# Gate matmuls spread over the last group's samples, and first queries and keys loaded into idle weight buffers

## The chip, the cores and the metric

The kernel runs on one core of a Trainium2 chip. The metric is the device time of one execution in microseconds (us), lower is better. The engines are TensorE (PE, with its weight loads as PEld), VectorE (DVE), ScalarE (ACT), GpSimd (POOL), and SyncE (SP), which only issues DMAs here.

## The reference

One inference step of a hybrid decoder layer, for a prompt of 1024 tokens and 8 x 4 sampled tokens (1056 tokens in all). Cut to what matters:

```python
proj = jnp.einsum('btd,de->bte', x, w_in)
c_q, c_kv, k_pe, z, xbc, dt_raw, g_logits = jnp.split(proj, IN_OFFSETS, axis=-1)
q_nope, q_pe, c_kv, k_pe = mla_project(...)
attn = attend(q_nope, q_pe, c_kv, k_pe)            # 16 heads, prompt causal; samples over a paged cache
ssm_out, new_conv, new_ssm = mamba2_branch(z, xbc, dt_raw, ...)   # state-space scan, 4 groups of 8 heads
gates = jax.nn.sigmoid(g_logits + b_gate)
merged = g_a * (attn @ w_branch_a) + g_b * (ssm_out @ w_branch_b)
h = layer_norm(ALPHA * x + merged @ w_out)
y = layer_norm(ALPHA * h + swiglu_ffn(h))
```

The state-space scan goes over the prompt in chunks; for each of the 8 samples the old state is read, multiplied with its decay, added to the samples' update and written back.

## The kernel before

The program has one hand-ordered instruction stream for each engine, tied by semaphores. Stages follow one another: projections of queries, keys and values (to about 254 us), the convolution tiles (to about 552 us), the state-space scan (to about 1147 us), attention of the prompt (to about 1460 us), attention of the samples, then branches, output and feed-forward.

**Thirds.** The dense products of the stage before (z and the gate logits: 32 units of 128 output columns over 1056 tokens) are spread through the scan. Each unit is cut in three *thirds* of 352 tokens; a third is 24 matmuls of 352 columns (`third`, line 1055 on TensorE). There are 96. Six (`LEAD`) come before the first group. Each of the 4 groups has 8 chunks of 128 tokens with two thirds each (lines 1172 to 1176), and then its samples (`ssm_samples`, line 1114), where `third_with(g, q)` (line 441) says whether sample q has a third: in groups 0 to 2 all eight have, in group 3 only q = 0 and 1. Every engine asks the same function. ScalarE takes each third out of PSUM with a Silu or Sigmoid (line 1745) and stores a finished unit (528 KB, line 1750). GpSimd splits each unit's raw weights in a high and a low part one unit ahead (`split`, line 746), SP loads the raw weights four units ahead into the four slots of `raw`.

**A sample.** TensorE: a third, if there is one; 16 matmuls of 4 columns with the turned old state (line 1136); four transposes of the next old state (line 1111); four products for the update (line 1147; each is two instructions in the trace). Between them ScalarE copies the turned state out of PSUM (`s_it`, line 1775), and VectorE forms the new state (`s_new`, line 2340), which ScalarE's queue stores. The next sample's line 1136 waits for the copy, and its line 1147 for the new state. SP loads the old states of q = 4 to 7 when the new states of q = 0 to 3 are out (line 567).

**Into attention.** When all 74 units are done (`unit_done` 74, line 620), SP loads the first two pairs of heads: for each pair two rotary key rows (`d_kr`, 128 KB each), two queries (384 KB), two keys and two values (256 KB each). The buffers `qb`, `kb`, `vb` (lines 402 to 410) lie over `xhi` and `xlo`, the tokens that every third reads. TensorE waits for `kr_full` (line 1185) and `head_full0`, computes the first pair's eight scores (line 1251), four before ScalarE has to read one (`probs`, line 1821). ScalarE first waits until all of its stores of the scan have landed (lines 1808 to 1815) and then signals `ssm_over`. DMA queue q1 is SP's, q10 ScalarE's. After the loop over pairs, SP loads the first weights of the branches into `raw` (line 682).

Of the kernel before, what the change touches and what calls it, by code (L numbers as in the profile page):

```python
# [16 lines left out]
D_MODEL, SEQ, NB, NT = 1024, 1024, 8, 4  # L17
# [3 lines left out]
HEADS, NOPE, ROPE, VH = 16, 64, 32, 64  # L21
QH = NOPE + ROPE
# [3 lines left out]
DI, SH, SP_, SG, SN = 2048, 32, 64, 4, 128  # L26
# [72 lines left out]
LEAD = 6  # L99
# [49 lines left out]
def build(nc, a, o, stop=99, debug=None):  # L149
# [22 lines left out]
    def sem(name):  # L172
        if name in taken:
            return sem(taken[name][0])
        if name not in sems:
            sems[name] = nc.alloc_semaphore(name)
        return sems[name]
# [22 lines left out]
    base = -(-nc.sbuf_base // 64) * 64  # L200
# [52 lines left out]
    d_kr = scratch("d_kr", [ROPE, TOK])  # L253
# [14 lines left out]
    ar = Arena(floor)  # L268
# [133 lines left out]
    qb, kb, vb = [], [], []  # L402
    ar = Arena(low)
    for pp in range(2):
        qb.append([ar(f"qb{pp}{h}", [QH, SEQ]) for h in range(2)])
        kb.append([ar(f"kb{pp}{h}", [QH, SEQ]) for h in range(2)])
        if pp == 1:
            assert ar.at <= at_wkv
            ar = Arena(at_kvt)
        vb.append([ar(f"vb{pp}{h}", [P, SEQ // P, VH]) for h in range(2)])  # L410
# [29 lines left out]

    def third_with(g, q):

        return g < SG - 1 or q < 8 - LEAD

    def step_of(g, c):

# [11 lines left out]
    def _(sp):  # L458
# [17 lines left out]
        def columns(n):  # L476
            return lambda r: r.rearrange("p (k n) -> p k n", n=n)

        def tile_of(w, col, n=P):
            return w[:, bass.ds(col, n)].rearrange("(k p) n -> p k n", p=P)  # L480
# [136 lines left out]
            return  # L617


        sp.wait_ge(sem("unit_done"), 74)  # L620
        for pp in range(2):
            for h in range(2):
                sp.dma_start(kb[pp][h][NOPE:QH, :], d_kr[:, 0:SEQ]).then_inc(sem("kr_full"), k["kr_full"].adds(16))

        one = lambda d, h: d[bass.ds(h, 1)].rearrange("a p n -> (a p) n")

        def queries_keys(pp, pair):
            for h in range(2):
                for dst, src in ((qb[pp][h][:, :], one(d_q, pair * 2 + h)[:, 0:SEQ]), (kb[pp][h][0:NOPE, :], one(d_k, pair * 2 + h))):
                    sp.dma_start(dst, src).then_inc(sem(f"head_full{pp}"), k[f"head_full{pp}"].adds(16))  # L630

        def head_values(pp, pair):
            for h in range(2):
                sp.dma_start(vb[pp][h][:, :, :].rearrange("p a n -> p (a n)"), one(d_v, pair * 2 + h)).then_inc(sem(f"head_full{pp}"), k[f"head_full{pp}"].adds(16))

        for pp in range(2):
            queries_keys(pp, pp)
            head_values(pp, pp)
        sp.wait_ge(sem("ssm_over"), 1)

        with nc.allow_non_contiguous_dma(reason="a page number for each quarter page, 4 KB in all"):
# [11 lines left out]
        with looped(sp, HEADS // 4 - 1, {k["s_ready"]: 32, k["o_ready"]: 4} | pairs(k, {"head_full": 96})) as i:  # L653
            for pp in range(2):
                sp.wait_ge(sem("s_ready"), k["s_ready"].next(16))
                queries_keys(pp, i * 2 + 2 + pp)
                sp.wait_ge(sem("o_ready"), k["o_ready"].next(2))
                head_values(pp, i * 2 + 2 + pp)
        if stop < 7:
# [10 lines left out]
        def gate_up(blk):  # L670
            return [[(columns(P), tile_of(w, blk * 256 + j * P))] for j in range(2) for w in (w_g, w_u)]

        def next_weights(n):
            for _ in range(n):
                weights(to_load.pop(0))
# [3 lines left out]
        for g in range(2):  # L679
            to_load += row_units(w_a, g * 512, 512, 256)  # L680
        to_load += [[(columns(P), tile_of(w_o, e * P))] for e in range(KT)] + gate_up(0)
        next_weights(4)
        sp.wait_ge(sem("olat_read"), 1 + NB - 1)

# [192 lines left out]
    def _(pe):  # L877
# [304 lines left out]
        for c in range(3):  # L1182
            pe.wait_ge(sem(f"third_free{c}"), k[f"third_free{c}"].next())
        pe.wait_ge(sem("xd_ready"), k["xd_ready"].next())
        pe.wait_ge(sem("kr_full"), k["kr_full"].next(64))
        pe.wait_ge(sem("bf_ready"), k["bf_ready"].next(2))

        def scores(pp, G, i):

            q, h, b = 4 * G + 3 - i // 2, i % 2, i % 2  # L1190
            if G == 0 and i == 0:
                pe.wait_ge(sem(f"head_full{pp}"), k[f"head_full{pp}"].next(96))
            first_bank = 2 * b + (i // 2 % 2 if G == 0 else 0)
            pe.wait_ge(sem(f"s_read{b}"), k[f"s_read{b}"].held() - (1 if G == 0 and i >= 2 else 0))
            length = (q + 1) * P
            for c in range(0, length, 512):
                w = min(512, length - c)
                pe.matmul(ps[:, first_bank + c // 512, 0:w], qb[pp][h][:, q * P:(q + 1) * P], kb[pp][h][:, c:c + w], start=True, stop=True)  # L1198
            at = q * P
            last = pe.matmul(ps[:, first_bank + at // 512, at % 512:at % 512 + P], ident_b[:, :], after_b[:, :], start=False, stop=True,  # L1200
                             skip_group_check=True)
            last.then_inc(sem("s_ready"), k["s_ready"].adds(1))
# [46 lines left out]
        per_two = {k["s_ready"]: 32, k["n_ready"]: 32, k["o_ready"]: 4} | pairs(k, {"head_full": 96, "s_read": 16, "pt_read": 24,  # L1249
                   "t_ready": 24, "o_read": 2})  # L1250
        for i in range(8):
            scores(0, 0, i)
        pe.wait_ge(sem("bt_read"), k["bt_read"].next())
        pe.wait_ge(sem("cb_read"), k["cb_read"].next())
        pe.wait_ge(sem("y_out"), k["y_out"].next())
# [1586 lines left out]
```

## Time and profile before

| | us |
|---|---|
| median of 3 runs | 3004.88 |
| lowest, highest | 2998.44, 3005.58 |
| profiled execution | 2995.18 |
| its span (first to last instruction) | 2993.3 |
| mean granted TensorE clock | 0.968 |

```profile
PE 2855.1 (95%) x18828; PEld 2562.1 (86%) x18828; DVE 1532.1 (51%) x2076; ACT 771.4 (26%) x1197; POOL 1024.6 (34%) x587
```

TensorE is busy 95% of the span. That is a mean over stages; the change touches the 600 us of the scan and its passage into attention, so it is those stretches that have to be read: which engine has idle time there, what ended it, and what clock TensorE was granted (1.00 is 2.4 GHz, 0.50 is 1.2 GHz).

### The profile page before, as it was taken

How to read it: one execution, taken by the hardware profiler on the slowest of the kernel's cores; microseconds unless marked ns; L12 is line 12 of the kernel's file. 1: busy time of each engine (PE TensorE's matmuls, PEld its weight loads, DVE VectorE, ACT ScalarE, POOL GpSimd, SP SyncE). 2: the span in 40 equal slices, each digit the busy share in tenths (PEclk: the TensorE clock that was granted, in tenths of full speed). 3: DMA queues.
4: the chain of work that ended last, by engine and by line, in shares of the span. 5: the costliest groups of instructions: out<-in, count | busy, mean ns of one | idle time of the engine just before them, and what ended most of it. 6: DMA issues, size and time to landing. Idle time of an engine off the chain costs nothing.

```text
span 2993.3 us, 45619 instructions
## 1 busy us (share of the span) xinstructions
PE 2855.1 (95%) x18828; PEld 2562.1 (86%) x18828; DVE 1532.1 (51%) x2076; ACT 771.4 (26%) x1197; POOL 1024.6 (34%) x587
## 2 busy tenths in 40 slices
PE   8899999999999998999999989999899999999996
PEld 7789999899989995555666689999799999999996
DVE  2774887664746554555344357865652222222227
ACT  1211221353535443555332222110220000000004
POOL 3543333332323322444211123444233333333330
PEclk9999999999999997999899989999899999999997
DMA  4154223574755535222334243353111111111101
GB/s 139 46 158 148 79 86 110 160 188 132 185 144 166 148 114 152 64 63 74 138 127 189 93 146 136 109 180 111 54 36 50 43 47 46 43 50 43 44 28 58
DMA packets 314166, 308.87 MB, mean 103 GB/s; under 512 B 31813, under 2 KB 272714, under 8 KB 311498
## 3 DMA queue, kind: packets, MB, share of 16 engines
q1 hardware_dynamic: 252008, 194.57, 22.9%
q10 hardware_dynamic: 58394, 73.89, 7.2%
q0 software_dynamic: 3584, 37.75, 3.3%
q8 instruction: 144, 2.36, 0.3%
q14 instruction: 36, 0.29, 0.0%
HBM read 227.96 MB, written 78.20 MB: 102 GB/s over the span
## 4 chain that ended last, share of the span: by engine, by line
PE 67%; DVE 12%; issue 10%; POOL 5%; ACT 4%; DMA 1%; SPq 0%; ACTq 0%; POOLq 0%; DVEq 0%
PE ps L908 41%; PE ps L1068 10%; POOL pr L854 4%; DVE cv L2199 3%; PE ps L1348 2%; PE ps L1324 2%; PE ps L1304 2%; DVE cv L2193 1%; PE ps L1147 1%; PE ps L1101 1%; DVE cv L2201 1%; PE ps L1105 1%; PE ps L979 1%; PE ps L1094 1%; ACT so L1696 1%
## 5 line engine op out<-in xcount | busy, mean ns | idle before, releaser
L751 POOL TENSOR_TENSOR whi<-raw,cst 128x1024 fp32r<-128x1024 f32 x160 | 312.0, 1950 | 1162.9 <-PE ps L908 959.9
L753 POOL TENSOR_TENSOR wlo<-raw,whi 128x1024 fp32r<-128x1024 f32 x160 | 431.2, 2695 | 12.6
L908 PE MATMUL ps<-ahi,whi 128*128 128x352 f32 x1728 | 376.4, 326 | 5.7 <-issue 3.5
L908 PE MATMUL ps<-alo,whi 128*128 128x352 f32 x1728 | 375.7, 326 | 0.0
L908 PE MATMUL ps<-ahi,wlo 128*128 128x352 f32 x1728 | 372.8, 324 | 0.0
L908 PEld LDWEIGHTS ps<-ahi,whi 128*128 128x128 f32 x1728 | 294.9, 190 | 7.4 <-issue 4.7
L908 PEld LDWEIGHTS ps<-ahi,wlo 128*128 128x128 f32 x1728 | 297.0, 190 | 0.0
L908 PEld LDWEIGHTS ps<-alo,whi 128*128 128x128 f32 x1728 | 295.5, 188 | 0.0
L1068 PE MATMUL ps<-xhi,whi 128*128 128x352 f32 x768 | 257.0, 335 | 0.6 <-ACT xraw L1693 0.4
L1068 PE MATMUL ps<-xhi,wlo 128*128 128x352 f32 x768 | 248.7, 324 | 0.0
L1068 PE MATMUL ps<-xlo,whi 128*128 128x352 f32 x768 | 248.6, 324 | 0.0
L854 POOL TENSOR_TENSOR pr<-pr,rowinv 128x384 f32<-128x384 f32 (+7 forms) x128 | 145.4, 1146 | 201.1 <-DVE rowinv L2402 201.1
L1198 PE MATMUL ps<-kb,qb 96*128 96x512 f32 (+3 forms) x384 | 160.4, 536 | 10.3 <-ACT pr L1827 6.9
L2397 DVE TENSOR_REDUCE negmax<-ps 128x1 f32<-128x384 f32 (+7 forms) x128 | 97.0, 758 | 136.9 <-PE ps L1200 136.2
L908 PE MATMUL ps<-xhi,whi 128*128 128x352 f32 x720 | 159.5, 330 | 6.0 <-ACT xraw L1693 3.9
L2583 DVE TENSOR_TENSOR mm<-ps,mm 128x1056 f32<-128x1056 f32 x80 | 100.6, 1258 | 116.3 <-PE ps L908 116.3
L908 PE MATMUL ps<-xlo,whi 128*128 128x352 f32 x720 | 158.1, 328 | 0.0
L908 PE MATMUL ps<-xhi,wlo 128*128 128x352 f32 x720 | 156.7, 327 | 0.0
L1198 PEld LDWEIGHTS ps<-kb,qb 96*128 96x128 f32 x384 | 65.1, 197 | 104.4 <-issue 83.5
L1068 PEld LDWEIGHTS ps<-xhi,whi 128*128 128x128 f32 x768 | 145.0, 189 | 9.2 <-issue 6.8
L1068 PEld LDWEIGHTS ps<-xlo,whi 128*128 128x128 f32 x768 | 145.1, 189 | 0.0
L1068 PEld LDWEIGHTS ps<-xhi,wlo 128*128 128x128 f32 x768 | 145.0, 189 | 0.0
(363 smaller groups left out, 5143.8 us busy)
## 6 DMA issues: line engine op xcount, KB each, us to landing
raw<-in_w_in SPq DMA_DIRECT2D x61, 512.0 KB, 5.1
s_a<-d_acum SPq DMA_DIRECT2D x32, 512.0 KB, 7.1
d_xbc<-so ACTq DMA_DIRECT2D x24, 528.0 KB, 2.7
gt<-d_g SPq DMA_DIRECT2D x24, 528.0 KB, 3.7
raw<-in_w_ffn_gate SPq DMA_DIRECT2D x22, 512.0 KB, 3.8
raw<-in_w_ffn_up SPq DMA_DIRECT2D x22, 512.0 KB, 3.8
raw<-in_w_ffn_down SPq DMA_DIRECT2D x22, 512.0 KB, 3.6
d_z<-zo ACTq DMA_DIRECT2D x16, 528.0 KB, 4.9
```

The costliest lines, as they stand in the source:

```text
L751: pool.tensor_tensor(whi[s][:, :], raw[:, u], ones[:, 0:1].broadcast_to([P, UNIT]), ALU.mult).then_inc(sem("unit_hi"), k["unit_hi"].adds(1))
L753: pool.tensor_tensor(wlo[s][:, :], raw[:, u], whi[s][:, :].bitcast(F32), ALU.subtract).then_inc(sem("unit_split"), k["unit_split"].adds(1))
L854: pool.tensor_tensor(pr[G][i][:, :], pr[G][i][:, :], rowinv[:, n:n + 1].broadcast_to([P, length]), ALU.mult).then_inc(sem("n_ready"), k["n ...
L908: last = pe.matmul(ps[0:m, 3 * b + c, 0:width], w(j), x[:, j, at:at + width], start=i == 0, stop=i == n - 1)
L1068: last = pe.matmul(ps[:, c, 0:CH], w[u % SPLIT][:, j * P:(j + 1) * P], x[:, j, c * CH:(c + 1) * CH], start=i == 0, stop=i == 3 * KT - 1)
L1198: pe.matmul(ps[:, first_bank + c // 512, 0:w], qb[pp][h][:, q * P:(q + 1) * P], kb[pp][h][:, c:c + w], start=True, stop=True)
L1304: last = pe.transpose(ps[:, 4 + i % 3, r * P:(r + 1) * P], src, ident)
L1324: last = pe.matmul(half(c, s), qcur[b][:, j, :], kvt[:, j, 4 * g:4 * g + 4, :].rearrange("p r n -> p (r n)"), start=False, stop=j == 1, sk ...
L1348: last = pe.matmul(ps[64 * s:64 * s + 64, 7, 0:KL], prt[:, 4 * c + r, 64 * s:64 * s + 64], kvb[b][:, 8 * r + 4 * s + c, :], start=r == c = ...
L2199: dve.scalar_tensor_tensor(out=cv[b][:, 0:SEQ], in0=xraw[b][:, j:j + SEQ], scalar=tap(j), in1=cv[b][:, 0:SEQ], op0=ALU.mult, op1=ALU.add). ...
L2397: dve.tensor_reduce(negmax[:, n:n + 1], src, AX, ALU.max, negate=True).then_inc(sem("m_ready"), k["m_ready"].adds(1))
L2583: dve.tensor_tensor(thirds(mm[:, e]), out3(b), thirds(mm[:, e]), ALU.add).then_inc(sem(f"res_free{b}"), k[f"res_free{b}"].adds(1))
```

## The change

In each of the groups 0 to 2 sample q = 3 has no third any more. The last group has thirds at q = 1, 3, 5, 6 and 7 in place of 0 and 1. The total remains 96, and the numbering of thirds in groups 1 to 3 shifts by one, two and three.

The query and key buffers of pair 0 are placed at the base of the memory, over the four slots of `raw`, and are filled when the last unit of weights has been split (`unit_split` 74) rather than when the last unit is done. The values of pair 0 and everything of pair 1 still wait for `unit_done` 74. TensorE's first eight scores wait for pair 0's rotary keys, queries and keys (`kr_full` 96), and for the values only after them. SP waits for all scores of pair 6 before it loads the first branch weights into `raw`.

```diff
-        qb.append([ar(f"qb{pp}{h}", [QH, SEQ]) for h in range(2)])
-        kb.append([ar(f"kb{pp}{h}", [QH, SEQ]) for h in range(2)])
+        qk = ar if pp else Arena(base)
+        qb.append([qk(f"qb{pp}{h}", [QH, SEQ]) for h in range(2)])
+        kb.append([qk(f"kb{pp}{h}", [QH, SEQ]) for h in range(2)])
...
     def third_with(g, q):
-        return g < SG - 1 or q < 8 - LEAD
+        return q != 3 if g < SG - 1 else q in (1, 3, 5, 6, 7)
...
-        sp.wait_ge(sem("unit_done"), 74)
-        for pp in range(2):
+        def rotary_keys(pp, name):
             for h in range(2):
-                sp.dma_start(kb[pp][h][NOPE:QH, :], d_kr[:, 0:SEQ]).then_inc(sem("kr_full"), k["kr_full"].adds(16))
+                sp.dma_start(kb[pp][h][NOPE:QH, :], d_kr[:, 0:SEQ]).then_inc(sem(name), k[name].adds(16))
...
-        for pp in range(2):
-            queries_keys(pp, pp)
-            head_values(pp, pp)
+        sp.wait_ge(sem("unit_split"), 74)
+        rotary_keys(0, "kr_full")
+        queries_keys(0, 0, "kr_full")
+        sp.wait_ge(sem("unit_done"), 74)
+        head_values(0, 0)
+        rotary_keys(1, "head_full1")
+        queries_keys(1, 1, "head_full1")
+        head_values(1, 1)
         sp.wait_ge(sem("ssm_over"), 1)
...
+        sp.wait_ge(sem("s_ready"), k["s_ready"].next(16))
         next_weights(4)
...
-        pe.wait_ge(sem("kr_full"), k["kr_full"].next(64))
+        pe.wait_ge(sem("kr_full"), k["kr_full"].next(96))
...
         for i in range(8):
-            scores(0, 0, i)
+            scores(0, 0, i, True)
+        pe.wait_ge(sem("head_full0"), k["head_full0"].next(32))
```

## Rows read from the trace of the kernel before

**Rows 1.** Windows: length; PE, PEld, DVE, ACT, POOL busy; clock, DMA share, GB/s.

```profile
964.00:1022.00 58.00, 58.00 (x486) 53.71 (x485) 20.80 (x52) 16.92 (x25) 10.63 (x7) 1.00 0.40 121
1108.00:1158.00 50.00, 43.50 (x311) 34.82 (x309) 15.05 (x49) 8.34 (x14) 0.00 (x0) 0.67 0.62 166
```

**Rows 2.** Timeline of TensorE, last group's samples: start, length, engine, line, operation.

```profile
1110.37 0.41 PE L1068 MATMUL ps<-xhi,whi 128*128 128x352 f32 x1
...
1114.40 0.64 PE L1136 MATMUL ps<-s_e,s_it 128*64 128x4 f32 x16
...
1116.63 0.43 PE L1068 MATMUL ps<-xhi,whi 128*128 128x352 f32 x1
...
1120.42 0.32 PE L1068 MATMUL ps<-xhi,wlo 128*128 128x352 f32 x1
1120.67 0.64 PE L1136 MATMUL ps<-s_e,s_it 128*64 128x4 f32 x16
...
1122.91 0.64 PE L1136 MATMUL ps<-s_e,s_it 128*64 128x4 f32 x16
...
1125.53 1.02 PE L1136 MATMUL ps<-s_e,s_it 128*64 128x4 f32 x16
...
1137.53 1.02 PE L1136 MATMUL ps<-s_e,s_it 128*64 128x4 f32 x16
...
1142.91 2.04 PE L1147 MATMUL ps<-s_bt,s_u 32*128 32x128 f32 x8 [0.35 <-DVE s_new L2340]
```

**Rows 3.** Timeline of ScalarE at the last group's first sample.

```profile
1110.65 0.60 ACT L1775 ACTIVATE s_it<-ps 128x512 f32<-128x512 f32 x1 [1.05 <-PE ps L1111]
```

**Rows 4.** Windows around two falls of the clock, columns as in rows 1.

```profile
449.43:451.59 2.16, 0.01 (x1) 0.03 (x1) 0.11 (x1) 1.61 (x2) 2.08 (x2) 1.00 0.35 139
451.59:452.66 1.07, 1.07 (x7) 1.07 (x8) 1.07 (x1) 0.00 (x0) 1.07 (x1) 1.00 0.57 225
452.66:456.00 3.34, 3.34 (x13) 3.34 (x13) 3.31 (x7) 0.00 (x0) 1.03 (x1) 0.50 0.36 83
...
1122.90:1125.00 2.10, 1.95 (x27) 1.71 (x27) 1.51 (x5) 0.26 (x1) 0.00 (x0) 1.00 0.32 133
1125.00:1129.50 4.50, 4.50 (x32) 3.73 (x30) 1.51 (x5) 0.94 (x2) 0.00 (x0) 0.51 0.68 186
```

**Rows 5.** Timeline of the DMA issues: first head load, last store of y.

```profile
1131.20 1.96 SPq L623 DMA_DIRECT2D kb<-d_kr  x4
...
1146.78 0.37 ACTq L1768 DMA_DIRECT2D d_y<-s_y  x1
```

**Rows 6.** Timeline of the passage into attention.

```profile
1147.46 2.05 PE L1198 MATMUL ps<-kb,qb 96*128 96x512 f32 x2 [2.52 <-DVE after_b L2377]
...
1156.09 1.28 ACT L1827 ACT_TABLE_LOAD   x1 [15.85 <-DMA d_y<-s_y]
...
1158.21 1.22 PE L1198 MATMUL ps<-kb,qb 96*128 96x256 f32 x2 [3.69 <-ACT pr L1827]
```

**Rows 7.** DMA traffic in 1132.7:1155.7, in 1135:1140 and in 1140:1144.

```profile
DMA packets 5102, 5.80 MB, mean 252 GB/s; under 512 B 880, under 2 KB 3819, under 8 KB 5099
...
DMA packets 338, 1.11 MB, mean 221 GB/s; under 512 B 68, under 2 KB 68, under 8 KB 338
...
DMA packets 1009, 1.28 MB, mean 320 GB/s; under 512 B 72, under 2 KB 646, under 8 KB 1007
```

**Rows 8.** Landings by line: queries and keys (L630), then y (L1768, two stores).

```profile
DMA to landing us min/median/max: 5.7/8.9/12.7
...
DMA to landing us min/median/max: 2.3/5.6/8.8
```

**Rows 9.** First branch weights: their issue on SP, and the splits on GpSimd.

```profile
1391.70 2.29 SPq L473 DMA_DIRECT2D raw<-in_w_branch_b  x4
...
L751 POOL TENSOR_TENSOR whi<-raw,cst x6: 1892/1894/1911, 1664.2 to 1794.9; 128x1024 fp32r<-128x1024 f32 x6
```

More of the change, by code:

```diff
@@ L617, in _, with queries_keys @@
             return
-        sp.wait_ge(sem("unit_done"), 74)
-        for pp in range(2):
+        one = lambda d, h: d[bass.ds(h, 1)].rearrange("a p n -> (a p) n")
+        def rotary_keys(pp, name):
             for h in range(2):
-                sp.dma_start(kb[pp][h][NOPE:QH, :], d_kr[:, 0:SEQ]).then_inc(sem("kr_full"), k["kr_full"].adds(16))
-        one = lambda d, h: d[bass.ds(h, 1)].rearrange("a p n -> (a p) n")
-        def queries_keys(pp, pair):
+                sp.dma_start(kb[pp][h][NOPE:QH, :], d_kr[:, 0:SEQ]).then_inc(sem(name), k[name].adds(16))
+        def queries_keys(pp, pair, name):
             for h in range(2):
                 for dst, src in ((qb[pp][h][:, :], one(d_q, pair * 2 + h)[:, 0:SEQ]), (kb[pp][h][0:NOPE, :], one(d_k, pair * 2 + h))):
-                    sp.dma_start(dst, src).then_inc(sem(f"head_full{pp}"), k[f"head_full{pp}"].adds(16))
+                    sp.dma_start(dst, src).then_inc(sem(name), k[name].adds(16))
         def head_values(pp, pair):
@@ L655, in _ @@
                 sp.wait_ge(sem("s_ready"), k["s_ready"].next(16))
-                queries_keys(pp, i * 2 + 2 + pp)
+                queries_keys(pp, i * 2 + 2 + pp, f"head_full{pp}")
                 sp.wait_ge(sem("o_ready"), k["o_ready"].next(2))
@@ L1184, in _, with scores @@
         pe.wait_ge(sem("xd_ready"), k["xd_ready"].next())
-        pe.wait_ge(sem("kr_full"), k["kr_full"].next(64))
+        pe.wait_ge(sem("kr_full"), k["kr_full"].next(96))
         pe.wait_ge(sem("bf_ready"), k["bf_ready"].next(2))
-        def scores(pp, G, i):
+        k["head_full1"].n = 32
+        def scores(pp, G, i, first=False):
             q, h, b = 4 * G + 3 - i // 2, i % 2, i % 2
-            if G == 0 and i == 0:
+            if G == 0 and i == 0 and not first:
                 pe.wait_ge(sem(f"head_full{pp}"), k[f"head_full{pp}"].next(96))
```

## The prediction

> **What bounds the kernel now.** I read three things in this order. First the busy time and granted clock by stage. In the samples of the third group TensorE is busy throughout and the clock is full; the first two groups' read alike, so one row stands for the three. In the last group's 50 us TensorE is busy 43.5 and the mean clock is 0.67 [rows 1]. So the other groups' samples are bound by TensorE, and the last group's are not. Second the timeline of that last stretch. A sample with a third takes 6.26 us from third to third (1110.37 to 1116.63), one without takes 2.62 (1122.91 to 1125.53) while the clock is full and 4.00 (1125.53 to 1137.53 is three) after it has fallen [rows 2]. The clock fell about 1125.1, some 4.5 us after the last third's matmuls ended, while TensorE was busy nearly all the time with short matmuls [rows 2, 4]. Third what ends the wait between the samples and attention. The first scores start at 1147.46 and fill the free banks; the next ones start at 1158.21, behind ScalarE's exponentials. ScalarE had idled 15.85 us until 1156.09, released by the landing of the last store of y, issued at 1146.78 and 8.8 us under way [rows 5, 6, 8]. That store lands so late because the DMA engines are full with the head loads and the stores of new states: 5.80 MB from 1132.7 to 1155.7 [rows 7]. Thus the end of the stage is set by a drain of DMA, not by the scores' own operands.
>
> **The thirds taken from the other groups.** Three thirds leave. At q = 3 of groups 0 to 2 a block of 6.26 becomes one of 2.62: 3 x 3.64 = 10.9 us off TensorE's path [rows 2]. What is late next in such a block is VectorE's new state, for which the update's matmuls wait some tenths of a microsecond, and ScalarE's copy of 0.60; both are in the 2.62 already [rows 2, 3]. The splits on GpSimd and the unit loads on SP move by one or two thirds with the count, but both are made three thirds ahead of use and there are two or three thirds' time under them; I cost them at nothing. If that cover were gone, a split would stand on the path, by its first half of 1.89 us [rows 9] and an estimated 2 to 3 for the second.
>
> **The thirds given to the last group.** It had thirds at q = 0 and 1 and gets them at 1, 3, 5, 6, 7. Before, the stretch from the first third (1110.37) to the end of the last update (1142.91 + 2.04 = 1144.95) is 34.6 us [rows 2]. After, at full clock: q = 0 has no third to hide the copy of the turned state, which ends at 1110.65 + 0.60 = 1111.25, so 0.9 us of stall [rows 3], then 2.23 for its own matmuls (1114.40 to 1116.63); four blocks with a third, 4 x 6.26 = 25.0; two without, 5.2; and the last one, 4.03 for the third and about 1.7 for the rest: 39.1 us. That is 4.5 more, and 10.9 - 4.5 = 6.4 us earlier at the end of the samples. In the old group's time scale the last third ends at 1147.8 and the samples at 1149.5; 10.9 is to be taken off both.
>
> **The first pair's loads.** Keys and queries of pair 0 (1.57 MB) go to the buffers of raw weights, after the last split instead of after the last unit. SP gets there only after the wait for the new state of q = 3, where it stood until 1131.20 in the kernel before too [rows 5]. In the changed kernel that is over 20 us ahead of the scores, against landings of 12.7 us at most [rows 8], so these loads are hidden. They compete with the stores of new states, whose buffers are used again only four samples later, 2 x 6.26 + 2 x 2.62 = 17.8 us. Nothing of this is gained by itself: the scores did not wait for their operands before either.
>
> **What is late next.** The other ten loads (values of pair 0, everything of pair 1: 2.62 MB) now wait for the last third, which is the last sample's. Behind that wait on SP's queue stand these ten and the page numbers; the first is needed by the first weighing, more than 10 us later, so the loads themselves are hidden. But they fall together with the last gate store (0.54 MB), the last new state (0.26) and y (0.07), all of which ScalarE waits for before its first exponential: 3.49 MB. From issue to flow was 1.5 us (1131.20 to 1132.7). The rate was 5.80 / 23.0 = 0.252 MB/us over the whole stretch, 0.222 from 1135 to 1140 and 0.32 from 1140 to 1144 [rows 7]. The first is nearest, since it too mixes loads and stores: 13.9 us, with ends of 10.9 and 15.7. So the drain ends at 1147.8 + 1.5 + 13.9 = 1163.2, less 10.9 = 1152.3, against 1146.78 + 8.8 = 1155.6 [rows 5, 8]: **3.3 us earlier**, with ends at 6.3 and 1.5. Half of the gain at the samples' end is lost to a longer drain. After it everything runs as before. The new wait of SP ahead of the weights of the next stage costs nothing: those loads were issued at 1391.70 and first split at 1664.2 [rows 9]; the wait puts them at most some tens of us later.
>
> **The clock.** This is the price that the trace does not settle. Taking a third away leaves a stretch of one sample's rest, 2.2 us, and a whole bare sample, 2.6: 4.8 us between the matmuls of two thirds. There are six: one in each of the groups 0 to 2, and before q = 1, 3 and 5 of the last (the first is 1.7 us of opening work plus 3.1). The 2.2 us stretches never cost the clock in the groups 0 to 2 [rows 1]. The one long stretch of the old kernel did, after 4.5 us [rows 2, 4]. Elsewhere the clock fell soon after a pause of only 2.16 us, though full-width matmuls had begun again 1.07 us before [rows 4]. So each of the six can fall, and none must. A fall is followed by 3.34 us at the half clock in the second case, in which 13 wide matmuls ran; at the third's pace (4.03 / 24 = 0.168 us) they take 2.2 us, so it lost 1.2; half of the stretch, 1.7, is the most. I take 1.4. The cost lies between 0 and 6 x 1.7 = 10.2 us; with half of the six falling it is 4.2.
> On the clock the Trainium skill ("TensorE: Matmul & The Clock Gate", section "Why this matters for your kernels") asks only that there be no idle gaps of some length between bursts. By that the six stretches, which are busy with short matmuls, would keep the full clock, and the sum would be that of the second case below. The trace speaks against reading it so: TensorE was busy 1.95 of 2.10 us just before the fall at 1125.1 [rows 4].
>
> **The sum.** -10.9 + 4.5 + 3.1 (longer drain) + 4.2 (clock) = +0.9 us. The profiled execution took 2995.18 us (span 2993.3, 1.9 around it), so 2996.1 by its own time. It lies 9.7 below the median of the three runs, 3004.88; I put the same difference on the median: **3005.8**.
>
> **The rivals.**
> - *Forecast, 0.50*: some of the six stretches lose the clock, the drain takes most of the rest: -1 to +4 around +0.9.
> - *The clock holds in all six, 0.22*: -3.3 us (-6.3 to -1.5 by the rates), 3001.6. For it: the short stretches of three groups held [rows 1]. Against it: the one of like length fell.
> - *The last stores are not held up by the loads, 0.12*: y is issued at 1149.5 + 1.8 - 10.9 = 1140.4 and lands 2.3 us later, as the one before it did [rows 8]; 1142.7 against 1155.6 is -12.9, so 2992.0. For it: fewer stores of new states are queued before it. Against it: in 1135 to 1140 the engines moved loads only, 338 packets, with stores outstanding [rows 7].
> - *Slower, 0.11*: all six stretches fall and the clock stays down through the whole third that follows, which then takes 4.03 us more. Six of these are 24.2, less 3.3: +20.9, 3025.8. It decides from four of the six on (16.1 - 3.3 = +12.8). For it: after the fall at 1125.1 the clock was still low at 1129.5, with TensorE busy throughout. Against it: it came back after 3.34 us of wide matmuls [rows 4].
> - *The change doesn't do what it says, 0.05*: the copy and update chains of the last group are slower with thirds between them, or the first pair's loads displace the states of the last samples, and the gain at the samples' end is gone: +3 to +6, about 3009. For it: the bare samples wait for VectorE. Against it: that wait is 0.35 us [rows 2].
>
> **The numbers.** What this kernel's measurement can tell from no change is about 0.3%, 9 us. The range reaches to half of the early-store case and takes in the milder part of the slow one: 2992 to 3014, which leaves out about 0.06 below and 0.10 above. Faster by over 0.3%: the early stores 0.12, the best end of the others 0.05, together 0.17. Slower: the slow case 0.11 and 0.03 of the forecast's and the last case's upper ends, 0.14. Same: 0.69.
>
> **What would show it.** At q = 3 of groups 0 to 2, blocks of 2.6 us between 6.26 ones; in the last group a stretch of 39 us from the first state copy to the last update, with full clock but for short falls; the drain step, in a y store that takes 10 us or more and ScalarE's first exponential some 13 us behind the last update (11 before). The clock step is wrong if the granted clock is 1.00 in all four groups' samples, or low for whole samples. The prediction fails if ScalarE's release comes within 6 us of the last update, or if chunk steps of the groups get longer than before, for which I found no reason.

## The result

| | time (us) | executions |
|---|---|---|
| before | 3003.09 (2991.70 to 3011.88) | 20 |
| after | 3014.35 (3007.76 to 3021.12) | 20 |
| after / before | 1.0037 [1.0028, 1.0047] | |

The change makes the kernel slower by 0.37%, some 11 us. 3005.8 was forecast, 0.9 us more than before; the measured time lies 0.35 us beyond the upper end of 3014, and slower had a chance of 0.14. The profiled execution of after took 3013.98 us (span 3012.2, mean clock 0.968).

The stretch that the change touches is read best by cutting it at the groups: each group's samples, from the turning of the state to the start of the last update, and the chunks between them. These are the windows of after in that cut (length; PE, PEld, DVE, ACT, POOL busy; granted clock, DMA share, GB/s). The rows of 46.90, 48.50, 50.00 and 44.00 are samples:

```profile
676.60:723.50 46.90, 46.75 (x413) 42.79 (x410) 15.71 (x41) 13.29 (x21) 10.57 (x5) 1.00 0.37 114
723.50:817.20 93.70, 91.93 (x709) 83.62 (x707) 66.66 (x95) 51.43 (x64) 33.99 (x18) 1.00 0.73 182
817.20:865.70 48.50, 48.34 (x414) 44.36 (x412) 19.25 (x41) 15.02 (x22) 14.80 (x7) 0.96 0.39 121
865.70:962.20 96.50, 93.46 (x706) 85.14 (x705) 65.85 (x95) 52.95 (x64) 34.05 (x18) 0.98 0.65 171
962.20:1012.20 50.00, 49.84 (x413) 45.78 (x410) 16.71 (x41) 13.94 (x21) 9.60 (x5) 0.93 0.38 117
1012.20:1105.40 93.20, 91.96 (x708) 83.65 (x707) 66.05 (x95) 52.86 (x64) 38.19 (x20) 1.00 0.55 146
1105.40:1149.40 44.00, 42.91 (x358) 39.14 (x356) 11.63 (x37) 7.99 (x14) 0.00 (x0) 0.88 0.43 121
```

And the same cut of a second profile of before (b1 below), of which the first two chunk stretches and the last group are enough; the samples of its other groups took 50.7 or 50.8 each at a clock of 1.00:

```profile
728.50:820.80 92.30, 91.90 (x707) 83.58 (x706) 66.80 (x95) 51.40 (x63) 38.91 (x20) 1.00 0.71 183
...
871.50:965.20 93.70, 91.94 (x709) 83.62 (x707) 66.56 (x95) 52.87 (x64) 38.18 (x20) 1.00 0.68 181
...
1108.40:1142.30 33.90, 33.39 (x286) 29.36 (x284) 11.63 (x37) 6.44 (x11) 0.00 (x0) 0.75 0.56 153
```

Three things are to be seen. The first group's samples show the gain without disturbance, 46.9 for 50.8; the next two have a lower clock and give part of it back. The last group takes 10 us more (44.0 for 33.9), at a clock of 0.88. And the chunks, in which nothing was changed, take 93.7 and 96.5 for 92.3 and 93.7.

The clock falls where the six stretches without wide matmuls are. In the last group of after, windows between the falls:

```profile
1105.40:1110.20 4.80, 4.02 (x54) 3.28 (x52) 1.47 (x3) 1.75 (x3) 0.00 (x0) 1.00 0.19 55
1110.20:1113.60 3.40, 3.40 (x13) 3.40 (x13) 1.51 (x5) 0.00 (x0) 0.00 (x0) 0.50 0.15 41
...
1115.70:1120.50 4.80, 4.64 (x58) 3.90 (x57) 1.51 (x5) 1.75 (x3) 0.00 (x0) 1.00 0.02 4
1120.50:1123.90 3.40, 3.40 (x13) 3.40 (x13) 1.51 (x5) 0.00 (x0) 0.00 (x0) 0.50 0.70 196
```

TensorE is busy 4.64 of 4.80 us with short matmuls, the clock then falls to its lower level (0.50, 1.2 GHz) just as the third's wide matmuls begin, and a good half of the third's 24 run at it. It is the same picture as in [rows 4], with 13 matmuls in the low stretch there and here; [rows 4] had it behind a pause. In this execution five of the six stretches ended so; the first one alone did not.

The passage into attention, timeline of ScalarE and TensorE in after:

```profile
1149.41 1.15 PE L1153 MATMUL ps<-s_bt,s_u 32*128 32x128 f32 x8
...
1152.39 0.49 ACTq L1777 DMA_DIRECT2D d_y<-s_y  x1
...
1159.85 1.28 ACT L1836 ACT_TABLE_LOAD   x1 [10.34 <-DMA d_y<-s_y]
...
1161.97 1.22 PE L1206 MATMUL ps<-kb,qb 96*128 96x256 f32 x2 [2.02 <-ACT pr L1836]
```

The last update starts 6.5 us later than in before ([rows 2], 1142.91), ScalarE is released 3.8 us later ([rows 6], 1156.09). The release is still set by y's landing.

### The profile page after: what moved, and what is told of

It reads as the page before. It is cut to its first block, busy times and chain, and to the rows that moved or that the text cites. A ratio compares the mean times of both kernels' runs of the same rounds, so it can differ in the third digit from the quotient of the medians.

```text
span 3012.2 us, 45617 instructions
## 1 busy us (share of the span) xinstructions
PE 2863.7 (95%) x18828; PEld 2563.1 (85%) x18828; DVE 1534.2 (51%) x2076; ACT 771.4 (26%) x1197; POOL 1023.4 (34%) x587
## 4 chain that ended last, share of the span: by engine, by line
PE 68%; DVE 12%; issue 10%; POOL 5%; ACT 3%; DMA 2%; SPq 1%; ACTq 0%; POOLq 0%; DVEq 0%
PE ps L914 40%; PE ps L1074 11%; POOL pr L860 4%; DVE cv L2208 3%; PE ps L1357 2%; PE ps L1333 2%; PE ps L1313 2%; PE ps L1107 1%; PE ps L1153 1%; DVE cv L2202 1%; PE ps L1111 1%; PE ps L1100 1%; DVE cv L2210 1%; PE ps L985 1%; ACT so L1705 1%
```

## The experiments

All profiles were cut in the same way. "Samples" are the four groups' samples, "chunks" the three stretches between them, "to last update" their sum, and "to samples' attention" the time from the last update's start to the first matmul of the attention of the samples. Times are medians, but for those marked (one), which are single executions. Ratios, with their 95% intervals, are to before, run at the same time on the same chip: e1 to e4, b1 to l2, c1 to c4, and d1 with d2 ran together. A ratio is an estimate of its own and differs by up to 0.0013 from the quotient of the two medians. The stretches are lengths and not points in time, because executions differ ahead of them too: the first group's samples open at 677.8 us in before and at 668.5 in p1, though the work up to there is the same.

| kernel | samples | chunks | to last update | to samples' attention | time (us) | ratio |
|---|---|---|---|---|---|---|
| before | 50.8 50.8 50.8 34.1 | 92.6 93.5 92.6 | 465.1 | 349.3 | 3003.09 | 1 |
| after | 46.9 48.4 50.0 44.0 | 93.7 96.6 93.2 | 472.8 | 346.4 | 3014.35 | 1.0037 [1.0028, 1.0047] |
| e1 after, shifted | 46.9 46.9 50.0 44.0 | 93.4 97.9 93.5 | 472.6 | 349.7 | 3014.75 | 1.0049 [1.0031, 1.0067] |
| e2 thirds alone | 48.5 49.8 50.0 45.5 | 93.6 96.3 93.6 | 477.3 | 357.8 | 3023.78 | 1.0072 [1.0052, 1.0091] |
| e3 buffers alone | 50.8 50.8 50.8 34.8 | 92.6 93.8 92.5 | 465.9 | 348.9 | 3004.66 | 1.0005 [0.9992, 1.0019] |
| e4 after again | 48.5 50.0 46.9 42.4 | 95.7 95.0 93.6 | 472.1 | 349.5 | 3008.57 (one) | |
| b1 before again | 50.8 50.8 50.8 33.9 | 92.3 93.7 92.5 | 464.6 | 349.8 | 3004.89 (one) | |
| p1 pieces, 21 and 15 | 46.9 46.9 46.9 38.5 | 93.5 96.9 93.3 | 463.0 | 351.1 | 3004.21 | 1.0007 [0.9996, 1.0017] |
| l1 old thirds, late loads | 50.8 50.8 50.8 33.5 | 92.6 95.5 93.0 | 466.9 | 344.6 | 2999.29 | 0.9989 [0.9973, 1.0005] |
| l2 after, late loads | 46.9 48.4 50.0 43.9 | 93.6 96.5 93.5 | 472.9 | 343.2 | 3005.62 | 1.0012 [0.9997, 1.0026] |
| c1 after, unit loads moved | 46.9 46.9 46.9 45.6 | 93.7 96.1 93.3 | 469.4 | 350.3 | 3009.73 | 1.0021 [1.0006, 1.0036] |
| c2 pieces, 24 and 6, late loads | 50.8 50.8 50.8 27.0 | 92.4 93.6 92.8 | 458.0 | 343.4 | 2989.63 | 0.9957 [0.9941, 0.9972] |
| c3 pieces, 21 and 15, late, moved | 46.9 46.9 46.9 38.5 | 93.3 96.4 93.2 | 462.1 | 343.8 | 2994.82 | 0.9972 [0.9957, 0.9987] |
| c4 before, third profile | 50.8 50.8 50.8 34.0 | 92.3 93.6 92.7 | 464.8 | 349.4 | 3003.03 (one) | |
| d1 pieces, 24 24 15 15, late | 50.8 50.8 39.7 38.5 | 92.5 93.4 93.2 | 458.9 | 344.1 | 2986.68 | 0.9944 [0.9923, 0.9965] |
| d2 pieces, 24 and 6 | 50.8 50.8 50.8 27.0 | 92.4 93.5 92.7 | 457.9 | 350.0 | 2993.95 | 0.9976 [0.996, 0.9992] |

**Each half alone, and a false lead.** Between the first profile of before and that of after, a second difference stood out far behind the change: in the attention of the samples, blocks of 64 short products took 1.28 us before and 2.86 after, in six of eight sequences. TensorE's instructions of after are one fewer, so a theory was that the whole stream's position matters. e1 shifts it back by one instruction, a wait that is long satisfied:

```diff
+        pe.wait_ge(sem("ident_full"), 16)
         pe.wait_ge(sem("late_full"), k["late_full"].next(96))
```

> The changed kernel with one idle wait more on TensorE, on a semaphore that is long there, just ahead of the attention of the samples; it puts every later TensorE instruction back by one place in its stream, to where it stood in the kernel before. Theory P (place in the instruction stream): the blocks of 64 short products of keys with rotary queries, which took 2.86 us each in the changed kernel's profile and 1.28 before, are back at 1.28; eight of them give back 8 x 1.6 = 12.8 us, so about 3014.4 - 12.8 = 3001.6, within 3 us of the kernel before. Rival M (the buffers' new place in memory, or the loads' new order, slow these products): nothing changes, some 11 us above the kernel before, blocks still 2.86 us.

e2 is before with the new distribution of thirds, e3 is after with the old one:

```diff
-        return g < SG - 1 or q < 8 - LEAD
+        return q != 3 if g < SG - 1 else q in (1, 3, 5, 6, 7)
```

> The kernel before with the new spread of thirds alone; buffers and order of loads as before, all twenty head loads (4.2 MB) behind the last third, and TensorE's instructions as many as before. Theory P: the short products stay at 1.28 us. The passage into attention gets later: in the changed kernel's profile attention's first exponential stood 5 us behind that of the kernel before (the 1.2 us by which that run was ahead at the start counted in); another 1.57 MB in the drain at 0.25 MB/us make 6 more, so +11 us in all, 3014. If the drain isn't what sets the end (rival), +3 to +6. A gain in the three bare blocks of 3.6 us each less what falls of the clock cost.

> The changed kernel with the old spread of thirds: first pair's queries and keys in the idle weight buffers, thirds at 0 to 7 in groups 0 to 2 and at 0 and 1 in the last. TensorE has the same one instruction fewer as the changed kernel. Theory P: the short products take 2.86 us, 12.8 us more in all; the passage into attention is as before, the head loads being gated by the same state store, so +12 to +13 us, 3016. Theory M expects the same here. If neither holds (a matter of one execution), 0.

e4 is after, unchanged:

> The changed kernel once more, for a second profile. If the slow short products belong to the program, all eight blocks take 2.86 us again; if to the execution, 1.28 in some. The falls of the clock in the six long stretches should come at other places, some three to five of them again.

The position theory fell: e1 has the blocks at 2.8 us, and the time of after. e2, e3 and e4 have the long blocks too, whatever their time. What was left was that the first profile of before had caught an uncommon execution, and a second profile of before (b1) was to settle it.

> The kernel before, unchanged, profiled a second time. In the first profile of it the blocks of 64 short products between the new states' samples in the stage after attention took 1.28 us in the sequences; in the kernel after, in both halves of the change alone and in the repeat of after they took 2.8 us in most. Theory 1 (a matter of the execution, not of the code): here too most take 2.8 us, that stage is some 10 us longer than in the first profile, and the profiled execution is close to the median, about 3003 us. Theory 2 (the change causes it): they take 1.28 us again in all, and the profiled execution is about 2995 us. In both the last update ends 572.6 us after the transposes that open the convolution.

It did. The same block, in the first profile and in the second one of before (timeline of TensorE; the 1.28 and 2.86 us count from the block's start to the next instruction, which is at 1521.73 and at 1523.17):

```profile
1520.44 1.35 PE L1319 MATMUL ps<-kpt,qcur 32*64 32x128 f32 x64
```

```profile
1520.31 1.31 PE L1319 MATMUL ps<-kpt,qcur 32*64 32x128 f32 x45
1521.95 0.46 PE L1319 MATMUL ps<-kpt,qcur 32*64 32x128 f32 x5 [0.33 <-issue]
1522.71 0.53 PE L1319 MATMUL ps<-kpt,qcur 32*64 32x128 f32 x14 [0.30 <-issue]
```

With the same code, the block is now broken twice by pauses for which the profile shows no cause. b1's execution took 3004.89 us and the first one 2995.18, and up to the samples' attention they agree within 0.5 us. c4 repeats it:

> The kernel before, profiled a third time, beside these three. Theory of two kinds of execution: the 64 short products in the attention of the samples take either 1.28 or 2.86 us in nearly all six inner places, the execution is 8 to 10 us shorter with the former, and everything up to that stage is the same within 1 us of the earlier two profiles when counted from the opening of the first group's samples (465 us to the last update).

It took 3003.03 us, with blocks of 2.86 and 464.8 us to the last update. The common execution is the one with pauses. The pauses are not all that makes executions differ: p1's profiled one took 2991.46 us, 13 below its median, and has them. Since the forecast carried the profile's distance of 9.7 us over to the median, this cost it nothing.

The halves: the buffers alone (e3) change nothing, as forecast. The thirds alone (e2) cost more than the whole change, and more than the 3014 expected: 12.2 us up to the last update and 8.5 behind it. There all sixteen head loads fall behind the last third, and the scores wait for them. Timeline of e2:

```profile
1149.23 1.73 SPq L623 DMA_DIRECT2D kb<-d_kr  x4
...
1165.98 2.04 PE L1198 MATMUL ps<-kb,qb 96*128 96x512 f32 x2 [15.13 <-DMA vb<-d_v]
```

So the second half of the change has a worth (8 to 11 us in the stretch to the samples' attention, 357.8 against 349.7, 349.5 and 346.4) that exists only with the first half.

**Is it the clock?** The thirds' wide matmuls were spread evenly over the samples, with the numbers of each group as in after:

```diff
-                if third_with(g, q):
-                    third()
+                some(21 if g < SG - 1 else 15)
```

where some(n) issues the next n of the 24 matmuls that make a third, and signals a third when its last one is issued.

> The kernel after, with the same number of thirds in each group but their wide matmuls spread evenly over the samples: 21 in each sample of groups 0 to 2, 15 in each of the last group, so that no stretch of 4.8 us is without wide matmuls. Theory clock (the stretches without wide matmuls cost the clock, about six falls of some 1.5 us, and they explain most of the miss): no low clock in the samples of any group, the last update ends some 8 us earlier against the opening of the convolution than in after (572 rather than 580), ScalarE's release with it, and the time is 3003 to 3007 us, 8 to 11 below after. Theory work (the last group's samples take longer for their own chain of copies and updates, and the groups' boundaries give back what the missing thirds saved, whatever the clock): the last group's samples still take 5 us longer than my sum, the last update ends at 577 to 581, and the time is 3011 to 3015 us.

Windows of p1, the last two groups' samples, and the chunks ahead of the second:

```profile
952.80:999.70 46.90, 46.90 (x413) 42.76 (x411) 16.16 (x41) 13.98 (x21) 9.62 (x5) 1.00 0.41 125
999.70:1093.00 93.30, 91.94 (x707) 83.64 (x705) 66.14 (x95) 52.86 (x64) 38.20 (x20) 1.00 0.55 146
1093.00:1131.50 38.50, 38.50 (x358) 34.37 (x355) 11.63 (x37) 8.00 (x14) 0.00 (x0) 1.00 0.52 138
```

The clock is 1.00 in all four groups' samples, TensorE is busy without a gap, and the same work to the last update takes 463.0 us instead of 472.8. The ratio falls by 0.0030, 9 us, and the intervals are apart. So the stretches without wide matmuls are the main part of the miss, and this run also shows the rest of the sum undisturbed: 46.9 in each group against 50.8, and 38.5 in the last. But p1 is not faster than before, although its samples are 7.3 us shorter in all (3 x 3.9 less 4.4): its chunks take 283.7 us instead of 278.7. They hold its one fall of the clock, 3.4 us at the start of group 2, behind a wait of TensorE of 3.42 us.

**The drain.** The ten loads of pair 0's values and of pair 1 were put behind the landing of the last y store, by moving one wait, in e3 (l1) and in after (l2):

```diff
         sp.wait_ge(sem("unit_done"), 74)
+        sp.wait_ge(sem("ssm_over"), 1)
         head_values(0, 0)
         rotary_keys(1, "head_full1")
         queries_keys(1, 1, "head_full1")
         head_values(1, 1)
-        sp.wait_ge(sem("ssm_over"), 1)
```

> The old spread of the gate thirds, the first pair's queries and keys in the idle buffers as in the change, and all of the other ten loads (values of pair 0, everything of pair 1, 2.62 MB) issued only behind the landing of the last y store. Theory drain (the loads that share the DMA engines with the last stores set ScalarE's release): the last y store takes 3 to 5 us rather than 9, ScalarE's first exponential comes 5 to 7 us sooner behind the last update, and the time is 2996 to 2999 us, 5 to 8 below the kernel before, as far as the values arrive in time. Theory values (what was saved at the release is lost at the first weighing, which then waits for its values, or at the second pair's scores): the release is earlier but the time is 3003 to 3006 us. Theory no drain: y still takes 9 us, and the time is that of the buffers alone, 3004.7 us.

> The kernel after, with the ten loads behind the landing of the last y store. Theory drain: as with the old thirds, 5 to 8 us below after (3006 to 3009 us), with a y store of 3 to 5 us. Theory values: no more than 2 us below after, 3012 to 3015 us, since the first weighing waits for its values. If the landing of y did not depend on the loads at all, y takes 7 to 10 us and the time is 3014 us.

Timeline of l1:

```profile
1148.66 0.46 ACTq L1777 DMA_DIRECT2D d_y<-s_y  x1
...
1151.39 1.28 ACT L1836 ACT_TABLE_LOAD   x1 [9.28 <-DMA d_y<-s_y]
...
1153.98 0.69 ACT L1836 ACTIVATE pr<-ps,negmax 128x512 f32<-128x512 f32 x1 [0.52 <-DVE negmax L2406]
```

y lands 2.2 us after its issue in both, against 8.8 in [rows 8] and 7.0 to 12.5 in the other kernels with early loads; ScalarE is released 6.6 us behind the start of the last update instead of 13.2 in before and 13.4 in e3. What is late next is VectorE's maxima behind the scores (the 0.52 in the last row), so of the 6.8 us that the release gains with the old thirds 4.3 arrive (348.9 to 344.6). With the new ones 3.2 to 6.5 arrive (from 346.4, 349.7 and 349.5 to 343.2). The ratios agree, 1.0005 to 0.9989 and 1.0037 to 1.0012, though only the second pair's intervals are apart. The values' late arrival was hidden: TensorE has no wait for them in l1.

**The chunks.** At a group's start TensorE waits for the decay sums (s_a) of a chunk, which come by DMA. At the start of group 1, the timeline of TensorE in before, then SyncE's issues and TensorE in after, then the same two in c1:

```profile
741.08 0.66 PE L1083 MATMUL ps<-cst,s_x 128*128 128x128 f32 x4 [0.67 <-DMA s_a<-d_acum]
```

```profile
730.15 0.43 SPq L565 DMA_DIRECT2D s_a<-d_acum  x1
730.63 0.79 SPq L474 DMA_DIRECT2D raw<-in_w_in  x1
```

```profile
737.16 0.66 PE L1089 MATMUL ps<-cst,s_x 128*128 128x128 f32 x4 [1.77 <-DMA s_a<-d_acum]
```

```profile
729.49 0.43 SPq L565 DMA_DIRECT2D s_a<-d_acum  x1
736.32 0.37 SPq L565 DMA_DIRECT2D s_x<-d_xbc  x1
```

```profile
736.53 0.66 PE L1090 MATMUL ps<-cst,s_x 128*128 128x128 f32 x4 [1.79 <-DMA s_a<-d_acum]
```

At the start of group 2 the wait is the longest, in before and in after (timeline of TensorE):

```profile
885.39 0.66 PE L1083 MATMUL ps<-cst,s_x 128*128 128x128 f32 x4 [1.63 <-DMA s_a<-d_acum]
```

```profile
880.57 0.66 PE L1089 MATMUL ps<-cst,s_x 128*128 128x128 f32 x4 [3.04 <-DMA s_a<-d_acum]
```

The three waits sum to 3.0 us in before and to 6.1 in after, and behind the 3.04 the clock is low for 3.4 us, from 881.5 on, which costs half of that: 3.1 + 1.7 is the 4.8 by which the chunks differ. The fall there is in all eight profiles with one third taken from each group (in e4 it is at the start of group 1), and in only one of the eight others, l1, whose second stretch is 95.5 for it.

At the start of group 1 the sums take 5.9 us from issue to landing in before and 7.0 in after. After has a weight load of 0.5 MB right behind the sums', since the units now fall at another place in the group. c1 puts SyncE's unit loads back to their old places:

```diff
-            if t % 3 == 0 and t // 3 + 4 < THIRDS // 3:
-                unit_of(NCONV + t // 3 + 4)
+            at = {b + (2 if 30 <= b < 51 else 1 if 51 <= b < 75 else 0): b for b in range(0, THIRDS, 3)}
+            if t in at and at[t] // 3 + 4 < THIRDS // 3:
+                unit_of(NCONV + at[t] // 3 + 4)
```

> The kernel after, with SyncE's loads of the gate's weight units put back to the places that they had in groups 1 and 2 (two thirds later in group 1, one third later in group 2), so that no 0.5 MB weight load is issued right behind the operands of a chunk step at the start of a group. Theory places (that load stretches the landing of the decay sums from 4.4 to 7.0 us and makes TensorE wait): the three stretches from a group's last update to the next group's turning of the state take 279 us together as in before, not 283.3 as in after, and the time is 3 to 5 us below after, about 3010 us. Theory VectorE (the chunk steps were not slack after the samples anyway, since the operands' buffers come free no earlier): the three stretches still take 283 us, and the time stays at 3014 us.

The next thing that SyncE issues behind the sums is now a chunk's operands, 6.8 us later; the wait is still there (1.79, and 2.68 at the start of group 2), and the chunks take 283.1 us. The load was not the cause. (The median fell by 5 us all the same; the intervals of the ratios overlap, and its profile had no fall in the samples of groups 0 to 2, where after had two.) What remains is that a group now begins at another place within a unit of three thirds, with all that goes with it. d1 keeps the place, by taking all three thirds from group 2:

```diff
-                some(21 if g < SG - 1 else 15)
+                some(24 if g < 2 else 15)
```

> Even pieces again, with the ten loads behind the landing of the last y store, but the three thirds that the last group gets all come from group 2: 24, 24, 15 and 15 wide matmuls in each sample. A unit of the gate is three thirds, so here every group begins at the same place within a unit as in before, while with one third from each group (21, 21, 21, 15) groups 1 and 2 begin at another. Theory place (at another place in the unit, the unit's own transfers, the 0.5 MB store above all, fall on the landing of the decay sums at a group's start): the three stretches between a group's last update and the next turning of the state take 279 us as in before, against 283 with 21, 21, 21, 15; samples 50.8, 50.8, 38.7 and 38.5; 457.5 us to the last update, and the time is 2989 to 2992 us. Theory rate (a group with fewer thirds reaches its boundary too early for VectorE or the DMA, wherever the unit stands): the stretch after group 2 takes 3 us or more above 92.6, the others are as before, 461 us to the last update.

Windows of d1, from the chunks of group 2 on:

```profile
862.80:956.20 93.40, 91.86 (x708) 83.56 (x705) 66.33 (x95) 52.87 (x64) 38.20 (x20) 1.00 0.67 182
956.20:996.00 39.80, 39.42 (x366) 35.19 (x364) 16.17 (x41) 12.60 (x19) 5.35 (x3) 1.00 0.39 114
996.00:1089.20 93.20, 91.93 (x707) 83.61 (x706) 66.04 (x95) 53.12 (x64) 38.20 (x20) 1.00 0.56 149
1089.20:1127.70 38.50, 38.50 (x358) 34.37 (x356) 11.63 (x37) 8.02 (x14) 0.00 (x0) 1.00 0.49 138
```

The chunks take 279.1 us, as in before, though group 2 has three thirds fewer. So missing thirds do not by themselves lengthen the stretch behind them. After's own third stretch says the same: three thirds are gone by then, the place within the unit is the old one again, and it took 93.2. What is left for the 4 to 5 us is the place within the unit. That is by elimination; no run moved the place alone. Which transfer does it is open. In after ScalarE issues the 0.53 MB store of a gate unit 3.3 us behind the sums' load (733.45 against 730.15) and in before 6.5 us ahead of it (728.68 against 735.17), and c1 left that store where it was; but no run moved it alone, and at the start of group 2 before too has a wait of 1.63 with its store 6.4 us ahead.

**What is best.** The last question was how much of this reaches the time together.

> Old numbers of thirds in each group, but in even pieces (24 wide matmuls in each sample of groups 0 to 2, 6 in each of the last group), with the first pair's queries and keys in the idle buffers and the other ten loads behind the landing of the last y store. By the other runs: samples of the last group 38.5 us with 15 in each, less three thirds of 4.03, 26.4 us against 34.0 in before, so the last update ends 7.6 us sooner than before if 6 wide matmuls in each sample keep the clock; the late loads give some 4 us more; 2990 to 2993 us beside before's 3001 to 3004. If 6 are not enough, the clock is low from the second sample of the last group on, the last group takes 34 us or more, and the time is 2998 to 3002 us.

> The even pieces of the new numbers (21 and 15), with the unit loads at their old places and the ten loads behind the landing of the last y store. From the even pieces alone (3004 us, ratio to before 1.0007): 4 us for the landing of y, 3 to 4 us for the group boundaries, so a ratio of 0.998 and 2996 to 2999 us. Rival: the two don't add up, as TensorE waits for the values at the first weighing or VectorE at the boundaries: 3001 to 3004 us.

> The old numbers of thirds in even pieces (24 and 6 in each sample), with the loads where the change puts them. It separates the two parts of the fastest kernel so far (2989.6 us). Theory sum: the pieces give 7 us (458 us to the last update, no low clock in the last group) and the late loads 4 us, so 2993 to 2996 us here, with y taking 9 to 12 us. Rival: the earlier last update only meets the same DMA drain, ScalarE's release comes no earlier than in before less 3 us, and the time is 2998 to 3001 us: then the two gains exist only together.

c2, with the old numbers, has a full clock through the last group, which takes 27.0 us where before takes 34.1:

```profile
1105.30:1132.30 27.00, 27.00 (x286) 22.86 (x284) 11.64 (x37) 5.91 (x11) 0.00 (x0) 1.00 0.60 160
```

d2, with early loads, still keeps its whole gain of 7 us at the last update, and the late loads give 6.6 more (350.0 to 343.4). In times that is 0.9976 and 0.9957, with intervals that overlap, so this second step rests on the profiles and on l1 and l2. c3 has the chunks at 282.9 (its unit loads are at the old places, as in c1) and lies between. c2 (2989.63 us) and d1 (2986.68) beat both before and after; their intervals overlap, so which of the two is better stays open. Moving thirds into the last group, which was the change's own step, is in d1 and not in c2, and to the last update they take 458.9 and 458.0 us. What the kernel could gain here was the granularity of the thirds and the order of the loads.

## Why the prediction was wrong

Step by step, in the order of the sum; the forecast of each, and what the runs show:

| step | forecast | measured | from |
|---|---|---|---|
| thirds off groups 0 to 2 | -10.9 | -11.7 | samples at full clock, 3 x (50.8 - 46.9) |
| last group, clock full | +4.5 | +4.4 | p1's 38.5 less 34.1, to the last update's start |
| clock | +4.2 | +10.1 | after less p1: 1.5 + 3.1 + 5.5 |
| group boundaries | 0 | +4.8 | chunks 283.5 less 278.7 |
| drain | +3.1 | +0.2, -2.9 | to samples' attention: e4 349.5, after 346.4, less 349.3 |

The forecast counts the last group to the end of the last update, the table to its start. The update takes 1.15 us at the full clock and 2.04 in before, so by the forecast's own cut 0.9 moves between two rows: the last group is +3.5, and the drain +1.1 in e4, +1.3 in e1, +2.7 in p1 and -2.0 in after.

**The main step that failed is the size of the clock term.** Its mechanism was right, and the price of one short fall too (1.4 forecast; 1.5 for the one in group 1, 1.8 in the mean of the three in the last group, where the fall begins with the third's own matmuls). The number was not: half of the six stretches were taken to fall, and five fell in after, e2 and l2, four in e1 and e4, three in c1. One of after's falls lasted 6.8 us and cost 3.1, more than the 1.7 that was held to be the most. So the term measured 10.1, the upper end that was given for it, and in e2, with four such long falls, 14.6. The evidence for falls was in the old trace: its only stretch of nearly five microseconds without wide matmuls fell, one of one. A further fall came at a group's start, behind the wait for the sums; it is in the next term.
The Trainium skill ("TensorE: Matmul & The Clock Gate", section "Why this matters for your kernels") asks only for the absence of idle gaps; by that these stretches would have kept the clock and the time would have been my second case, 3001.6. The traces don't agree with that: the clock fell after a stretch in which TensorE was busy 4.64 of 4.80 us.

**The second is the group boundaries, costed at nothing.** I had written that splits and unit loads "move by one or two thirds with the count" and are made three thirds ahead, and looked only at whether they are in time. They were. What I left out is what else runs at that place: at a group's start TensorE already stood 0.7 to 1.6 us for a chunk's operands in the old trace, at each of the three starts, so anything that delays their landing there is on the path. A shift by one third made these 1.8, 3.0 and 1.2 us, and the longest has a fall of the clock behind it. "Chunk steps of the groups get longer than before, for which I found no reason" was named as what would make the prediction fail. It is what happened.

**The drain was over-sized by 0.4 to 2 us, and by 5 in the profiled execution of after,** counted from the end of the last update (+3.1 forecast). Its mechanism held: l1, l2, c2, c3 and d1 show that the loads set y's landing. y took 10.4 us in e1 and e4 and 7.0 in the profiled execution of after, and ScalarE's release came 12.7, 12.7 and 9.3 us behind the end of the last update, where 10 and some 13 were named as what would show the step. So in two of three executions the landing itself was as forecast. What it cost against before was less: the passage from the last update's start to the samples' attention took 349.7 and 349.5 us against 349.3, and 346.4 in after. Why y landed in 7.0 us in that one is open. The early-store case of -12.9 did not come about, as the loads were still early.

The rest was right. The thirds' own sum came to -7.3 against -6.4 (-8.2 to the end of the last update). The buffers are worth nothing by themselves (e3), and the weights of the next stage, the extra wait of SyncE and the splits cost nothing that shows. To the last update the terms as measured sum to -11.7 + 4.4 + 10.1 + 4.8 = 7.6, against 472.8 - 465.1 = 7.7 in the profiles. With e4's passage this makes +7.9 us, where the medians differ by 11.3 and the interval of the ratio allows 8.4 to 14.1: half a microsecond at the least, and 3.4 by the medians, stay unexplained. The stretch behind the start of the samples' attention doesn't hold them steadily: it took 1516.4 us in after, but 1510.3 in e1 and 1509.7 in e4, against 1511.0 and 1511.5 in b1 and c4.

Of the rivals, the slower one was nearest in its mechanism: it had all six fall and the clock stay low through whole thirds, +20.9. The falls were nearly as many, but shorter. Its threshold ("decides from four of the six on") was met in after, e1, e2, e4 and l2, at 1.5 to 3.5 us for each fall where it had 4.03.

## What to carry to other kernels

Filler work that keeps TensorE's clock up was worth more here in small even pieces than in whole blocks with pauses between: the same matmuls as 21 and 15 in each sample gave 9 us over whole thirds, and 6 in each sample kept a clock that two whole thirds had lost. When a count changes, ask where the periodic transfers that follow the count will now fall, not only whether they are in time. And when an engine's release hangs on a small last store, look at which large loads are issued ahead of it that nobody needs yet: holding ten loads back made it land in 2.2 us instead of 9.0 (l1 against e3).

## What the hardware showed

- The clock fell with TensorE busy 4.64 of 4.80 us, when nearly all of it was short matmuls, and came back after 3.4 or 6.8 us of mostly wide ones. Whether one stretch ends in a fall differs between executions of one kernel: the stretch in group 0 fell in e4 and not in after, that in group 2 the other way round.
- A store of 64 KB took 2.2 or 2.3 us from issue to landing in the five kernels whose last ten head loads (2.6 MB) came later, and 7.0 to 12.5 us in the eleven profiles in which SyncE issued them around it.
- 64 short products took 1.28 or 2.86 us in executions of one and the same kernel, the longer ones broken by pauses of 0.3 us in the issue; nearly all profiles, 15 of 16, show the longer form, and the difference is most of the 9.7 us by which one execution of before was below its median. No run here told what sets it.
